# Moving the second layer's weight sums, two weight splits and the pair sums in a two-layer streaming encoder on one core

## The reference, cut to what matters

```python
def layer(x, ...):                        # run for DEPTH = 2 layers, D_MODEL = 1024
    h = rmsnorm(x, g_pre_mix)
    z = h @ w_in                          # [B | C | xin | c_q | c_kv | k_rope | gate_conv | gate_mla]
    yc, new_buf = short_conv(c_g * xin, conv_buf, conv_w)
    y_a = b_g * yc
    q = (rmsnorm(cq, g_q) @ w_uq)         # 8 heads of 128 + 64 rotary
    ckv_new = rmsnorm(ckv_raw, g_kv)
    kpe_new = apply_rope(kpe_raw, cos, sin)
    y_b = mla_attention(...)              # softmax over k, chunk mask
    merged = sigmoid(ga) * y_a + sigmoid(gb) * y_b
    x = x + rmsnorm(merged @ w_o, g_post_mix)
    f = jnp.square(jax.nn.relu(rmsnorm(x, g_pre_ffn) @ w1)) @ w2     # D_FF = 4096
    x = x + rmsnorm(f, g_post_ffn)
```

## Time and profile before

| | us |
|---|---|
| median of three executions | 1719.85 |
| the profiled execution's own time | 1719.35 |
| its span, first to last instruction | 1717.5 |
| PE busy | 1704.5 |
| DVE busy | 1313.3 |
| ACT busy | 862.5 |
| POOL busy | 122.3 |

### The profile page before, as it was taken

One profiled execution on the slowest core, in us unless ns is written; L12 is line 12 of the kernel. 1 busy time (PEld: TensorE's weight loads), 2 busy tenths in 40 slices (PEclk: granted clock), 3 DMA queues, 4 the chain that ended last, 5 costly groups with the idle time before them and its releaser, 6 DMA issues.

```text
span 1717.5 us, 31904 instructions
## 1 busy us (share of the span) xinstructions
PE 1704.5 (99%) x12735; PEld 1690.0 (98%) x12735; DVE 1313.3 (76%) x2512; ACT 862.5 (50%) x1669; POOL 122.3 (7%) x163
## 2 busy tenths in 40 slices
PE   9999999999999999999999999999999999999997
PEld 9999999999999999999999999999999999999997
DVE  7788877767798777668688788777678887777665
ACT  7636454544554544446366364545446636444452
POOL 1412222122200000000000000000000000000000
PEclk9999999999999999999999999999999999999999
DMA  7888989898842323233133234443433313322231
GB/s 240 199 191 181 230 207 216 188 265 214 175 110 63 111 82 92 87 98 99 62 119 123 90 116 128 116 127 114 162 118 99 99 39 110 99 87 87 74 99 56
DMA packets 85619, 222.09 MB, mean 129 GB/s; under 512 B 9568, under 2 KB 21088, under 8 KB 85472
## 3 DMA queue, kind: packets, MB, share of 16 engines
q1 hardware_dynamic: 66592, 176.01, 32.1%
q0 software_dynamic: 17600, 41.95, 13.8%
q10 hardware_dynamic: 1280, 2.10, 0.4%
HBM read 209.67 MB, written 52.30 MB: 153 GB/s over the span
## 4 chain that ended last, share of the span: by engine, by line
PE 95%; DVE 3%; DMA 1%; issue 1%; ACT 0%; SPq 0%; DVEq 0%; ACTq 0%
PE ring L817 19%; PE ring L819 19%; PE ring L818 19%; PE att L817 11%; PE att L819 11%; PE att L818 11%; DMA w_raw<-blocks_in 1%; PE att L3589 1%; DVE w_lo L2092 1%; PE att L812 1%; PE att L811 1%; PE att L824 0%; PE att L3405 0%; PE att L825 0%; PE att L3744 0%
## 5 line engine op out<-in xcount | busy, mean ns | idle before, releaser
L817 PE MATMUL ring<-xs_hi,w_lo 128*128 128x288 f32 x1872 | 556.5, 297 | 1.2 <-DVE w_lo L2092 0.5
L819 PE MATMUL ring<-xs_hi,w_hi 128*128 128x288 f32 x1872 | 551.5, 295 | 0.0
L818 PE MATMUL ring<-xs_lo,w_hi 128*128 128x288 f32 x1872 | 551.3, 294 | 0.0
L2092 DVE TENSOR_TENSOR w_lo<-w_raw,w_hi 128x1024 fp32r<-128x1024 f32 (+1 forms) x364 | 370.8, 1038 | 38.7 <-ACT w_hi L1209 28.6
L817 PEld LDWEIGHTS ring<-xs_hi,w_lo 128*128 128x128 f32 x1872 | 351.6, 188 | 3.9 <-DVE w_lo L2092 1.3
L818 PEld LDWEIGHTS ring<-xs_lo,w_hi 128*128 128x128 f32 x1872 | 351.8, 188 | 1.4
L819 PEld LDWEIGHTS ring<-xs_hi,w_hi 128*128 128x128 f32 x1872 | 351.6, 188 | 0.0
L819 PE MATMUL att<-f_hi,w_hi 128*128 128x288 f32 x960 | 283.2, 295 | 0.0
L818 PE MATMUL att<-f_lo,w_hi 128*128 128x288 f32 x960 | 282.9, 295 | 0.0
L817 PE MATMUL att<-f_hi,w_lo 128*128 128x288 f32 x960 | 282.6, 294 | 0.0
L817 PEld LDWEIGHTS att<-f_hi,w_lo 128*128 128x128 f32 x960 | 180.4, 188 | 0.0
(11 more groups left out here) (346 smaller groups left out, 3189.9 us busy)
## 6 DMA issues: line engine op xcount, KB each, us to landing
w_raw<-blocks_in SPq DMA_DIRECT2D x197, 512.0 KB, 3.7
weight_sums<-blocks_in POOLq DMA_DIRECT2D x80, 256.0 KB, 7.1
w_raw<-blocks_in SPq DMA_DIRECT2D x58, 256.0 KB, 4.1
weight_sums<-blocks_in POOLq DMA_DIRECT2D x20, 512.0 KB, 5.4
weight_sums<-weight_sums POOLq DMA_DIRECT2D x40, 256.0 KB, 7.6
w_raw<-weight_sums SPq DMA_DIRECT2D x20, 512.0 KB, 4.6
w_raw<-weight_sums SPq DMA_DIRECT2D x40, 256.0 KB, 4.2
small_raw<-small_in SPq DMA_DIRECT2D x16, 320.0 KB, 4.0
```

Of the source, the lines that this page charges most:

```text
L817: pe.matmul(out, w[1], x[0], start=first, stop=False)
L818: pe.matmul(out, w[0], x[1], start=False, stop=False)
L819: return pe.matmul(out, w[0], x[0], start=False, stop=last)
L2092: return dve.tensor_tensor(out, a, hi.bitcast(F32), ALU.subtract)
```

## The change

Four pieces of code move and one wait is added. POOL makes only the first layer's ten sets of weight sums in its first call; then it waits until PE has finished the first product of pair (2, 1) of layer 0, in the feed-forward part, and makes the second layer's ten sets there. In the first mixed head of both layers DVE and ACT split position `at + 2` later, and DVE position `at + 3` later still. In `outs_and_lo` DVE makes the pair sums ahead of the two rests of f and the two tile reads that stood before them. The orders of PE and of SP are unchanged.

```diff
--- before.py
+++ after.py
@@ -1181,7 +1181,11 @@
             key_rope(L, 0)
             key_rope(L, 1)
             if L == 0:
-                sums_steps(BEFORE_KEYS, N_SUMS + 2, 0, N_SUMS)
+                sums_steps(BEFORE_KEYS, 2 * MIXED + 2, 0, 2 * MIXED)
+                pool.wait_ge(pl.sums_third, 16 * 2 * MIXED)
+                pool.wait_ge(pl.ring_full, full(0, r_pair(2, 1, 0)))
+                sums_copy(2 * MIXED)
+                sums_steps(2 * MIXED, N_SUMS + 2, 2 * MIXED, N_SUMS)
         for i, (m0, m1) in enumerate(TAIL_MOVED):
             pool.wait_ge(pl.tail_factored, i + 1)
             nc.gpsimd.tensor_tensor(pl.x[:, m0:m1, cols(1)], pl.x[:, m0:m1, cols(1)], pl.last[:, m0:m1, :], ALU.add) \
@@ -1602,7 +1606,6 @@
                     values_hi(h, 0)
                     values_hi(h, 1)
                     if h == FIRST_MIXED:
-                        pos_hi(L, at + 2)
                         turned_hi_of(3)
                     else:
                         pos_hi(L, at + 3)
@@ -1630,6 +1633,7 @@
                     turned_hi_of(0)
                     snapshot(0)
                     even_projections()
+                    pos_hi(L, at + 2)
                     block_kept(0)
                     pos_hi(L, at + 3)
                     block_kept(1)
@@ -2684,10 +2688,7 @@
                     values_lo(h, 0)
                     values_lo(h, 1)
                     if h == FIRST_MIXED:
-                        pos_lo(L, at + 2)
                         head_mix_lo(2)
-                        pos_lo(L, at + 3)
-                        head_mix_lo(3)
                     else:
                         pos_lo(L, at + 3)
                     query_lo(h, 0)
@@ -2701,7 +2702,10 @@
                     upper_left(0, pl.cv[:, cols(0)])
                     normed_head_lo(3)
                     even_projections()
+                    pos_lo(L, at + 2)
+                    head_mix_lo(3)
                     first_difference(0)
+                    pos_lo(L, at + 3)
                     second_sum(0)
                     conv_state(h)
                     lower_left(0, pl.u[:, 2:2 + NH])
@@ -3163,11 +3167,11 @@
 
             def outs_and_lo(g, k0, g0, p0, g1, p1):
 
+                pair_sums(g1, p1)
                 f_done(g0, p0, 2)
                 w2_out(g, k0)
                 f_done(g0, p0, 3)
                 w2_out(g, k0 + 1)
-                pair_sums(g1, p1)
                 lo_a22(g1, p1)
                 lo_s3(g1, p1)
                 w2_out(g, k0 + 2)
```

## The result

The changed kernel takes 1729.27 us in the median of six executions (1727.53 to 1730.65); with seven more on record the range is 1727.53 to 1736.4. Six executions of the kernel before on the same chip took 1719.6 us in the median (1718.69 to 1726.58). The ratio is 1.0057, 95% interval 1.004 to 1.0075: slower by 0.57%, 9.7 us. I had forecast 1723 us, a range of 1718.5 to 1729, and no measurable change.

What follows compares the result with a forecast made beforehand. The kernel was taken as bound by PE's number of matmuls, PE being 99% busy. Terms -0.8 + 2.4 + 1.8 = +3.4 us on 1719.35 gave 1722.7, about 1723 with 0.5 us to the median; range 1718.5 to 1729.

Steps and rivals of the forecast that it cites:

- The limit of 5.9 us for a second block: Feed-forward part, new order: a load landing later than 5.9 us after issue makes PE wait for the excess.
- The 6.8 us of the old order: Feed-forward part, pair sums behind the tile reads: a landing up to 6.8 us after issue moved nothing at all.
- the 0.8 us for the heads of layer 0: Heads of layer 0 without layer 1's sums: loads come earlier, a gain of 0.8 us.
- the whole price of making all 20 sets of sums in layer 0: Heads of layer 0: 0.83 us lost against layer 1, taken as all that PE can see in this stretch.
- tile reads behind late loads: Layer 0's feed-forward part: eight pieces lose 0.3 us each, 2.4 us in all; low end 0, high end 30.
- The forecast's own sign of being wrong: Prediction is wrong if PE loses more than 8 us at 606 to 800 us, in layer 0's feed-forward part.
- the third rival: Layer 0's feed-forward part: second blocks landing 7.5 us after issue cost 16 us, about 1737 us in all; chance 0.09.
- The head's term: First mixed head: later weight positions delay products 2 and 4, 0.9 us a layer, 1.8 in all; range 0.6 to 1.2 a layer.
- The first (loads in time): Feed-forward part: loads stay in time beside the moved sums, +1.0 us, about 1720.5 us; chance 0.22.
- The second (only the recovered 0.8 us): First mixed head: its new order costs nothing, only -0.8 us remains, about 1718.7 us; chance 0.13.
- The fourth: Sums come too late for layer 1's rotary key at 897.29 us; given nothing worth counting.
- a landing of at most about 5.2 us: Feed-forward part: one load beside one POOL stream lands within about 5.2 us, making the tile-read loss 0.

Runs made afterwards that it cites:

- the run with SP's late loads: Kernel before, with the pair sums ahead of the two tile reads and SP's load of the second block issued two tiles later: 1738.9 us, ratio 1.0109.
- the run with late loads in the old order: Kernel before, only SP's load of the second block issued two tiles later, pair sums still behind the two tile reads: 1720.94 us, ratio 1.0007.
- the one with ACT's edit: Changed kernel, but ACT makes the high part of the next pair's first block behind three high parts PE wants first: 1727.17 us, ratio 1.0043.
- the one with half the sums: Changed kernel, but five of layer 1's ten sets are made in layer 0's heads and five in the feed-forward part: 1725.04 us, ratio 1.0024.

## Why the prediction was wrong

*Right:* what bounds the kernel, and that the change can only open or close gaps of PE. Product 2 starts 0.09 us behind DVE's split and loses 0.85 to 0.93 us, forecast 0.86. POOL's last issue comes at 813.64 us, forecast near 800. The limit of 5.9 us for a second block held to 0.1 us in five traces with POOL's DMAs and in the run with SP's late loads. The 6.8 us of the old order are on the safe side, since PE's own limit there is near 7.6. Layer 1's feed-forward part lost nothing. The sign of the sum was right.

*Right by luck:* the 0.8 us for the heads of layer 0. In the two profiles that are compared it came out to 0.05 us, and the layers are the same distance apart at both places. But "the whole price of making all 20 sets of sums in layer 0" was read from one execution, and that price is not fixed: three kernels with all 20 sets in the heads do not pay it at that place, and the average of six is 0.4 us.

*Wrong:* the step that failed is the term "tile reads behind late loads", 8 x 0.3 = 2.4 us. It measured 11.4 us in the first profile of the changed kernel and 7.4 in the second. By the medians it is about 7.5 us: 9.7, plus the 0.4 that the heads give back on average, less 2.6 for the two first mixed heads. Some 4.5 of them come without the new order of DVE. The forecast's own sign of being wrong, a loss of more than 8 us there, came in the first profile. Three things made it too small.

1. The landing. I took that of 60 to 240 us, 4.8 us in the median, because the loads come one by one there too. Measured were 5.6 to 6.4 us in the seven profiles with all ten sets in this part. I had one second block in three late by about 1 us. Late were 3, 4 and 4 of 8 in the three traces with the new order that are taken apart above, by 2.0, 1.1 and 1.5 us on average: 5.9, 4.5 and 6.2 us of PE (the changed kernel, the same again, the one with ACT's edit).
2. The second path. I followed only DVE's queue and only the second block. The first block reaches the same tile read through ACT's queue: 3.4 us in the first profile, 2.2 in the second. I had named a "late first block" in the third rival alone, and not followed it. A third path, the block of the second matrix that ACT splits ahead of f, was not named at all; with the old order it cost up to 2.2 us in one piece.
3. The statement that before the change a landing up to 6.8 us "moved nothing at all" is true of a second block (the run with late loads in the old order) and was taken for all loads. So I held the moved sums harmless without the new order, and they cost 0.21% by themselves.

The lower clock behind some waits is a fourth, 1.5 us in three of the profiles.

The head's term was 0.9 us a layer and measured 1.28 to 1.37, above my high end of 1.2. I had product 4 wait 0.1 us; it waits 0.4, as `first_difference` waits for PE (0.71 us, to 163.56) before the last split can begin. This term and the one above were each too small, the gain in the heads was too large, and all three errors have one sign.

*The rivals.* The first (loads in time) fell: in all seven traces with the ten sets here PE waited for tile reads, and lost 2.6 us at the least. The second (only the recovered 0.8 us) fell with product 2. The third had the forecast's mechanism at twice the measured size: its 16 us needed a mean landing of 7.5 us. The fourth did not occur; POOL stood idle for 94.9 us before the rotary key.

The Trainium skill, "DMA: Bandwidth & Descriptors", section on queues, rings and completion order, has the DMA engines serve their queues in turn, packet by packet, from which I had estimated a landing of at most about 5.2 us beside POOL's stream. The traces disagree with that estimate: the median lies above it, and the latest load took 9.6 us in the first profile and 10.7 in another. Whether the rule itself fails is not shown, since no view here tells whom a DMA engine served when. What the estimate added to it was one single stream beside the load, and a fixed part of about 2 us that the page fits for DMAs of POOL and not of SP.

*What stays open:* why one load takes 3.6 us and the next 9 beside the same kind of neighbour was not tried, nor whether a single load split over several issues would land sooner. How the loss of the moved sums divides between the three loads rests on single traces and on ratios whose intervals overlap. Nor was it tried why the same DMAs of POOL in the heads cost PE 0.8 us in one execution and nothing in another.

## What to carry to other kernels

When a change puts traffic beside loads that were early, list every engine whose queue waits for each of those loads, not only the one whose order is edited, and take the slack of each from the trace as issue to latest harmless landing; then compare it with the tail of the landings, since the mean costs nothing and the tail all. An edit that is free by itself (here the pair sums first: 1.0001) can cost 2 to 4 us beside another, when it spends the cover that the other needs. And a work item moved from a stretch whose DMA engines are busy to one where they are idle gains only what PE had lost in the first, however busy that stretch looks. That loss has to be read from more than one execution: here one trace had 0.8 us, three others none.

## What the runs showed of the hardware

**A half-speed stretch behind a short wait.** Behind waits of 1.90, 2.43 and 2.78 us (the changed kernel, the one with ACT's edit, the one with sums and pair sums) PE ran 13 to 15 matmuls 240 ns apart, at the lower level of 1.2 GHz, for about 3 us; in one of them at once, in two after eight or nine matmuls at 132 ns. That costs about 1.5 us each time. Behind waits of 2.77 and 3.35 us in other pieces it did not happen, nor behind any wait of up to 1.82 us. What else decides was not tried. The stretches of the kernel with ACT's edit (behind 2.43 us) and of the one with half the sums (behind 2.77 us):

```profile
735.00:742.00 7.00, 7.00 (x41) 7.00 (x42) 6.67 (x13) 1.06 (x1) 1.67 (x3) 0.76 0.57 124
```
```profile
689.00:696.00 7.00, 6.87 (x52) 6.87 (x52) 6.98 (x15) 1.07 (x2) 1.64 (x2) 1.00 0.65 123
```

The page's mean clock (0.997) hides it, and so does the busy time: in the first of these PE counts as busy for all 7.00 us with 41 matmuls in place of 55.

**Loads beside accumulating DMAs.** A load of 512 KB that lands in 3.4 to 3.6 us when POOL is silent took 5.6 to 6.4 in the median and up to 10.7 beside POOL's copies and adds in DRAM, although the DMA engines were 0.79 busy and not full.
